# Conv inputs, q, k and v by seven-product iterations ahead of the gates, and attention inside the pool and conv projection

## The reference, cut to what matters

```python
h = _rmsnorm(x, norm1)
proj = einsum('bsd,de->bse', h, w_in)          # 2048 -> 11336 columns
(u_pool, c_b, c_c, c_x,                        # 512 columns each
 q, k, v,                                      # 1024 each: 8 heads of 128
 qi, ki, wi, gate_logits) = split(proj)        # 512, 64, 8, 6144
a = _multiscale_pool(u_pool, pool_w, pool_scale)
bconv = c_b * causal_conv3(c_c * c_x)          # along the tokens, per channel
q = _rmsnorm(q.reshape(B, S, 8, 128), q_gain)  # k likewise
c = _sparse_attention(q, k, v, qi, ki, wi * 8 ** -0.5, topk=128)
g = sigmoid(gate_logits).reshape(B, S, 3, D)
merged = g0 * (a @ w_pool_out) + g1 * (bconv @ w_conv_out) + g2 * (c @ w_attn_out)
x = x + merged @ w_o
x = x + square(relu(_rmsnorm(x, norm2) @ w_ff1)) @ w_ff2
```

## Time and profile before

| | us |
|---|---|
| median of three runs | 2642.54 |
| span of the profiled execution | 2643.3 |
| PE busy (2623.1 us) | 99% of the span |
| DVE busy (1949.0 us) | 74% |
| ACT busy (1241.7 us) | 47% |
| DMA, mean | 216 GB/s |

### The profile page before, as it was taken

One profiled execution on the slowest core, in us unless ns is written; L12 is line 12 of the kernel. 1 busy time (PEld: TensorE's weight loads), 2 busy tenths in 40 slices (PEclk: granted clock), 3 DMA queues, 4 the chain that ended last, 5 costly groups with the idle time before them and its releaser, 6 DMA issues.

```text
span 2643.3 us, 36093 instructions
## 1 busy us (share of the span) xinstructions
PE 2623.1 (99%) x14114; PEld 2255.0 (85%) x14114; DVE 1949.0 (74%) x2293; ACT 1241.7 (47%) x1615; POOL 94.5 (4%) x116
## 2 busy tenths in 40 slices
PE   8999999999999999999999999999999999999999
PEld 6688877777888888888889999999999788888887
DVE  4565654567777775477569888888887988888887
ACT  6322344335444543234566665656655433333333
POOL 0022222100000000000000000000000000000000
PEclk9999999999999999999999999999999999999999
DMA  7589999956445557556775566566568777685753
GB/s 242 174 230 247 252 254 255 275 175 236 161 160 175 175 175 271 165 169 219 251 231 174 174 211 209 166 218 198 171 219 326 256 273 251 215 318 182 273 188 121
DMA packets 317973, 570.76 MB, mean 216 GB/s; under 512 B 20137, under 2 KB 128297, under 8 KB 317297
## 3 DMA queue, kind: packets, MB, share of 16 engines
q1 hardware_dynamic: 272688, 433.64, 49.4%
q0 software_dynamic: 20736, 58.73, 9.9%
q10 hardware_dynamic: 24384, 76.18, 7.8%
HBM read 476.05 MB, written 151.01 MB: 237 GB/s over the span
## 4 chain that ended last, share of the span: by engine, by line
PE 91%; DVE 4%; DMA 3%; issue 1%; ACT 1%; SPq 0%; ACTq 0%; DVEq 0%
PE aux L1182 8%; PE aux L1184 8%; PE aux L1183 8%; PE main L1286 7%; PE main L1288 7%; PE main L1287 7%; PE main L1182 6%; PE main L1184 6%; PE main L1183 6%; PE main L511 5%; PE main L513 5%; PE main L512 5%; PE main L1217 1%; PE aux L1217 1%; PE aux L1218 1%; PE aux L1219 1%
## 5 line engine op out<-in xcount | busy, mean ns | idle before, releaser
L1286 PE MATMUL main<-sf,f_wh 128*128 128x256 f32 x1728 | 489.3, 283 | 1.1 <-ACT keeps L1773 0.9
L1287 PE MATMUL main<-sf,f_wh 128*128 128x256 f32 x1728 | 489.0, 283 | 0.0
L1288 PE MATMUL main<-sf,f_wl 128*128 128x256 f32 x1728 | 489.0, 283 | 0.0
L1286 PEld LDWEIGHTS main<-sf,f_wh 128*128 128x128 f32 x1728 | 331.7, 192 | 1.8 <-ACT keeps L1773 1.3
L1288 PEld LDWEIGHTS main<-sf,f_wl 128*128 128x128 f32 x1728 | 331.7, 192 | 0.0
L1287 PEld LDWEIGHTS main<-sf,f_wh 128*128 128x128 f32 x1728 | 331.7, 192 | 0.0
L486 DVE TENSOR_TENSOR w_lo<-w_raw,w_hi 128x512 fp32r<-128x512 f32 (+1 forms) x184 | 123.2, 674 | 207.6 <-ACT w_hi L479 206.5
L479 ACT ACTIVATE w_hi<-w_raw 128x512 fp32r<-128x512 f32 (+1 forms) x184 | 113.1, 617 | 269.3 <-PE main L513 209.0
L511 PE MATMUL main<-act_hi,w_hi 128*128 128x512 f32 x576 | 229.9, 399 | 8.0 <-DVE w_lo L486 7.9
L1473 ACT ACTIVATE f_wh<-group 128x1024 fp32r<-128x1024 f32 x128 | 135.7, 1061 | 204.9 <-PE aux L1184 104.1
L513 PE MATMUL main<-act_hi,w_lo 128*128 128x512 f32 x576 | 225.2, 391 | 0.0
(11 more groups left out here) (311 smaller groups left out, 5887.0 us busy)
## 6 DMA issues: line engine op xcount, KB each, us to landing
group<-w_ff SPq DMA_DIRECT2D x160, 512.0 KB, 5.2
f1raw<-w_ff SPq DMA_DIRECT2D x126, 512.0 KB, 5.7
sf<-f_dram ACTq DMA_DIRECT2D x56, 1024.0 KB, 11.7
group_g<-w_in SPq DMA_DIRECT2D x100, 512.0 KB, 4.6
w_raw<-w_in SPq DMA_DIRECT2D x87, 512.0 KB, 8.2
f_dram<-piece_hi SPq DMA_DIRECT2D x112, 256.0 KB, 4.0
f_dram<-piece_lo SPq DMA_DIRECT2D x112, 256.0 KB, 5.1
t_dram<-w_o POOLq DMA_DIRECT2D x48, 512.0 KB, 8.2
```

The source lines that it names most:

```text
L1286: pe.matmul(part, hi_at(8, k)[:, cols], sh, start=first, stop=False, skip_group_check=True)
L1287: pe.matmul(part, hi_at(8, k)[:, cols], sl, start=False, stop=False, skip_group_check=True)
L1288: mm = pe.matmul(part, lo_at(8, k)[:, cols], sh, start=False, stop=last, skip_group_check=True)
```

## The change

Four iterations J = -4 to -1 are put ahead of the gates: `J_CONV` makes c_c and c_x, `J_Q`, `J_K`, `J_V` make q, k, v. c_b stays plain (two passes, 16 units), which now follow the pool passes. The index scores move 9 units later, the pool product and its spill into the c_b passes. The `h` block sums are made during the index passes and `h_dram` is gone; J = 0 is an ordinary iteration; POOL's sets are 10, one for each 16 granules from granule 28 on. z = c_c c_x is multiplied with tokens on partitions; z, q and k are then turned by PE (80 transposes of 128 by 128) and spilled, v is scaled and spilled. The squares of q and k heads are summed by ACT, eight activations of 128 columns with a sum for each block where a gate block has two of 512. Top-k, masks and the convolution go between the `lo2` of the gate iterations. The gate blocks `gb` have one set of buffers, not two. The branch order becomes pool and conv for all four chunks (32 units), then attention for all four (32 units); the heads run one in four units from unit 5 on. Pool and conv segments after the first all use `main`, since attention holds `aux`.

```diff
+    J_CONV, J_Q, J_K, J_V = -4, -3, -2, -1
+    J0 = J_CONV
...
-        gb = [[at(f"gb{p}_{i}", [P, 2, S], F32, o * KB) for i, o in enumerate(at_kb)]
+        gb = [at(f"gb{i}", [P, 2, S], F32, (128 + 4 * i) * KB) for i in range(4)]
...
+        SEGS = [(ci, b) for ci in range(4) for b in range(2)] + [(ci, 2) for ci in range(4)]
+        SEG_END = [4 * s + 3 for s in range(8)] + [39 + 8 * i for i in range(4)]
...
+        def weight_cols(J):
+            if J < 0:
+                return ((c_c, PW), (c_q, S), (c_q + AW, S), (c_v, S))[J - J0]
+            return c_gate + (J % 3) * D + (J // 3) * S, D // 2
```

SP at the start of the branches (and the PE order of the iterations and branches):

```diff
+            sp.wait_ge(g_done, KO + 28 * 6)
             load_sig(0)
+            sp.wait_ge(vm_spilled, 80)
+            sp.dma_start(maskB[:], mask_dram).then_inc(rows_landed[6], 16)
             load_sig(1)
+            sp.wait_ge(vm_spilled, 64)
+            sp.dma_start(vv[:], v_dram.rearrange("t p c -> p t c")).then_inc(rows_landed[5], 16)
             next_sig = 2
             for g in range(u_b + 8, u_w, 2):
                 load_b(g)
...
-            for J in range(6):
-                for n, g in order_of(J):
+            for J in range(J0, 6):
+                for idx, (n, g) in enumerate(order_of(J)):
                     granule(J, n, g)
+                    if J == J_Q and idx in (5, 7):
+                        for i in range(2):
+                            turn_block(idx - 5 + i)
+                    if J in (J_K, J_V) and idx in (3, 5, 7):
+                        for i in ((0, 1, 2, 3), (4, 5), (6, 7))[(idx - 3) // 2]:
+                            turn_block(tile_0(J) + i)
...
+            for ub in range(4 * KT):
+                a = ub - ATTN_AT
+                h, s = a // 4, a % 4
+                if 0 <= a <= 4 * ATTN_HEADS and s == 0:
+                    if h:
+                        pv(h - 1)
+                    if h < ATTN_HEADS:
+                        logits(h)
+                if 0 <= a < 4 * ATTN_HEADS and s == 3:
+                    turns(h)
...
+                branch_unit(ub)
```

ACT: the end of an iteration, and the way of the k factors through DRAM:

```diff
-            def sigmoid_gate(J, i):
+            def finish_gate(J, i):
+                if J == J_CONV:
+                    return
...
+                    if J in (J_Q, J_K):
+                        for c in range(4):
+                            n = 32 * (J - J_Q) + 8 * i + 4 * j + c
+                            col = 4 * (8 * (J - J_Q) + 4 * v + c) + t
+                            if n >= 2:
+                                act.wait_ge(hq_squared, n - 1)
+                            act.activation(head_junk[n % 2][:], gb[blk][:, j, c * P:(c + 1) * P], ACT.Square,
+                                           accum_out=ss64[:, col:col + 1]).then_inc(hq_squared, 1)
...
+                    if J == 1 and idx == 0:
+                        act.wait_ge(k_ready, 1)
+                        act.dma_start(k_dram.rearrange("h (t p) -> p h t", p=P),
+                                      rqk[:, 32:64].rearrange("p (h t) -> p h t", t=TT),
+                                      allow_slow_non_contiguous=True).then_inc(k_moved[0], 16)
...
+                if ub == 1:
+                    load_k_factor(0)
+                    load_k_factor(1)
```

DVE: the end of the plain passes, what is put between the granules' splits, and the branches:

```diff
+            def cb_evict(i):
+                dve.wait_ge(unit_done, (6 + i) * UP)
...
+                for m in range(2):
+                    ins = dve.tensor_tensor(cbT[i][:, m], main[:, bank + m, :], rB[:, :], ALU.mult)
...
+            cb_evict(1)
...
+            TOP_AT = [(J, idx) for J in range(J0, 2) for idx in (6, 9, 11, 13, 15, 17, 19) if J > J0 or idx > 6]
+            def mixers_after(J, idx):
+                if (J, idx) in TOP_AT:
+                    pick_top(UP - 1 + TOP_AT.index((J, idx)))
...
+                if J == 2 and idx in (9, 13, 17):
+                    chain.step(mask((idx - 9) // 4))
+                if J in (3, 4) and idx in (9, 14):
+                    convolve(2 * (J - 3) + (idx == 14))
...
+            mix_t1(J0, 0)
+            for J in range(J0, 6):
                 for g in range(4):
                     lo2(J, 0, g)
...
+                if ub == 3:
+                    scale_k(0)
+                if ub - 1 in SEG_END[:8] and SEGS[SEG_END.index(ub - 1)][1]:
+                    merge_sums(SEG_END.index(ub - 1))
...
+                if ub in SEG_END:
+                    merge(SEG_END.index(ub))
```

POOL:

```diff
-            for n in range(14 + 3):
-                    pool.wait_ge(lo_ready, u_qk + 8 * n)
+            for n in range(10 + 3):
+                    pool.wait_ge(f_lo, 28 + 16 * n)
```

More of the change, by code:

```diff
@@ L754, in _ @@
                 load_b(g)
-                while next_sig < 12 and 4 * next_sig + 4 * (next_sig // 3) <= (g - u_b - 8):
+                while next_sig < 12 and SEG_END[next_sig - 2] + 4 <= g - u_b - 8:
                     load_sig(next_sig)
@@ L1214, in _ @@
                 pe.wait_ge(lo_ready, g + 1)
                 for t in range(TT):
+                    if first and s >= 2 and s != 10:
+                        pe.wait_ge(gate_mul, 4 * (9 if s == 11 else s - 1) + t + 1)
                     th, tl = brT[:, kt, 0, t * P:(t + 1) * P], brT[:, kt, 1, t * P:(t + 1) * P]
@@ L1606, in _ @@
                     gates_after(J, idx)
+                    if J == J_Q and idx in (9, 12):
+                        for i in range(2):
+                            tile_out((idx - 9) // 3 * 2 + i)
+                    if J in (J_K, J_V) and idx in (6, 7, 9, 12):
+                        for i in range(2):
+                            tile_out(tile_0(J) + 2 * (6, 7, 9, 12).index(idx) + i)
+                    if J == 0 and idx == 8:
+                        act.wait_ge(ms_ready, 2)
+                        act.activation(rqk, ms64, ACT.Sqrt).then_inc(root_done, 1)
@@ L1968, in pool_group, with clear_scores @@
                                   ALU.subtract).then_inc(pool_diff, 1)
-            for g in range(u_idx, u_qk):
+            def clear_scores():
+                dve.wait_ge(score_added, 24)
+                for i in (1, 2, 3):
+                    chain.step(dve.memset(score[i - 1][0:CHUNK, i * P + CHUNK:(i + 1) * P], EMPTY))
+                chain.wait()
+                for i in (1, 2, 3):
+                    chain.step(dve.tensor_copy(work[i - 1][:], score[i - 1][:]))
+                chain.wait()
@@ new lines, in pick_top @@
+            def pick_top(pair):
+                t = pair % 3
+                chain.step(dve.max(top8[t], work[t][:]))
+                chain.wait()
+                chain.step(dve.match_replace(work[t][:], top8[t], work[t][:], EMPTY))
+                chain.wait()
+            def cb_evict(i):
+                dve.wait_ge(unit_done, (6 + i) * UP)
+                if i == 0:
+                    dve.wait_ge(score_added, 24)
+                    dve.wait_ge(pool_diff, NW)
+                else:
+                    dve.wait_ge(a_spilled[0], 64)
+                bank = 2 * (1 - i)
+                for m in range(2):
+                    ins = dve.tensor_tensor(cbT[i][:, m], main[:, bank + m, :], rB[:, :], ALU.mult)
+                ins.then_inc(cb_ready, 1)
+                dve.wait_ge(cb_ready, i + 1)
+                dve.sem_inc(set_free[1 - i], 1)
@@ L2056, in mask @@
                 kth = top8[t][:, 7:8]
[L2057 removed]
+                above, equal, rank = dst, work[t][:], score[t][:]
                 chain.step(dve.tensor_scalar(above, score[t][:], kth, None, ALU.is_gt, ALU.add,
@@ new lines, in convolve @@
+            def convolve(m):
+                if m % 2 == 0:
+                    dve.wait_ge(conv_landed, 16 * m + 32)
+                if m == 0:
+                    dve.wait_ge(vm_spilled, 80)
+                else:
+                    dve.wait_ge(b_lo, m)
+                tap = [cst[:, C_CW + 4 * k + m:C_CW + 4 * k + m + 1] for k in range(CONV_K)]
+                chain.step(dve.tensor_scalar(yc[:], zz[:, m % 2, 0:S], tap[0], None, ALU.mult))
+                for k in range(1, CONV_K):
+                    chain.wait()
+                    chain.step(dve.scalar_tensor_tensor(yc[:], zz[:, m % 2, k:k + S], tap[k], yc[:], ALU.mult, ALU.add))
+                chain.wait()
+                dve.tensor_tensor(yc[:], yc[:], cbl[:, m % 2], ALU.mult).then_inc(b_ready, 1)
```

1367 lines of the change are left out of this document (616 added, 751 removed).

## The result

The changed kernel takes 2653.4 us (median of 4) where the kernel before takes 2643.0: the ratio is 1.004, with an interval from 1.0028 to 1.0053. So it is slower by 10 us where I forecast 33 us less.

What follows compares the result with a forecast made beforehand. The prediction took PE as the bound, busy 2623.1 of 2643.3 us. Its terms, -43.6 - 7.3 + 9.1 - 3.6 + 5.7 + 3.2 + 3.0, gave -33.5 us: 2609 us, range 2603 to 2616 (0.60), eight in ten 2599 to 2625.

Steps and rivals of the forecast that it cites:

- scattered write: J = 1, k factors written as 4096 single floats: 36 us to land, delaying a copy 7 us (2616); chance 0.04, taken as 0.
- GpSimd's rounds: POOL's block-sum sets beside group loads in J = -3 to 2: no cost in the sum, a cost only if DMA fills up.
- sign that I had named for being wrong: Either `g_wl` waits all over the gates (DVE or DMA late), or a wait at every head.
- What PE has to do: Matmuls removed and added net -43.6 us, squares' sums -7.3 us, turns of tiles +9.1 us.
- Turns: 80 transposes on PE for 20 tiles: 0.105 us each, 8.4 us, plus 0.7 for matmuls behind groups, together +9.1 us.
- Old stalls that go: Gates, nearly all in J = 0, 2.8 us of stall and 0.8 for the spill of h disappear: -3.6 us.
- Start of J = -4: First granule waits for DVE's c_b products, sum and low part: 4.0 us idle plus 1.7 from low clock, 5.7 us.
- Squares on ACT: End of J = -3 and -2: eight squares take 3.1 us, 1.9 more than two sigmoids; PE loses 3.2 us in all.
- DVE's added work in the iterations: Top-k, masks and convolution between splits: DVE 86 to 88% busy, covered by the splits' lead, costed at nothing.
- Branches and later heads: Head 0 waits behind k factor, merge and unit 8's weights: 3.0 us (first 1.4); later heads add nothing.
- DMA fills up: Group loads beside POOL's sets in J = -3 to 2: 57 loads late by 1.1 us each, 63 us, 2672; chance 0.04.

Runs made afterwards that it cites:

- k_before: Kernel before the change plus the same write of 4096 single floats on ACT's queue at J = 1, read by nobody: 2650.6 us, ratio 1.0025.
- a_kturn: Changed kernel with k factors turned by DVE in 32 x 32 blocks and written as 128 runs of 128 bytes: 2639.5 us, ratio 0.9983.
- c_wo: Changed kernel with W_o's first four weight blocks ahead of the reloads of x in SP's queue: 2643.7 us, ratio 0.9997.
- g_all: Changed kernel with five mends (k write, W_o order, unit 8's weights, J = -4 start, spread GpSimd DMAs) and two k factors fetched earlier: 2602.3 us, ratio 0.9842.
- f_spread: Changed kernel with the eight DMAs of each GpSimd round issued one per two granules, not all at once: 2634.7 us, ratio 0.9971.

## Why the prediction was wrong

The step that failed is the pricing of DMAs beside the iterations and ahead of W_o. The sum has 0 for the scattered write ("As small as that data is, I take 0") and 0 for GpSimd's rounds, and no term for the reloads of x ahead of W_o's weights. The runs showed 17.1 us of loss at the write and a round beside it, 19.9 at two bursts of the rounds and 8.9 at W_o. Neither sign that I had named for being wrong showed: `g_wl` waits stand in four places and not all over the gates, and no later head waits. Term by term:

**What PE has to do: right.** The first and the last matmul are 9.4 us further apart than before, the loss grew by 56.7, so by this count the work shrank by 47.3 where the sum had 41.8. The difference is no gain. The line of the index scores mixes three shapes, and its median is 0.289 us before and 0.157 after, though its 48 instructions take 10.9 us together before and 10.2 after. With one price for each kind and shape in both kernels the work shrank by 42.6 us and the loss grew by 52.0. Turns came at 0.109 us each.

**Old stalls that go: right at least.** By that count the loss outside the places of the table fell by 9.3 us where I had 3.6. Most of the rest is a stall that nothing in the change aims at and that I don't explain: from 2000 us on, in the MLP, the loss is 5.0 us before, around the wait of the earlier trace rows, and 0.6 after.

**Start of J = -4: right in mechanism and size.** 4.1 us of wait, then half the clock, 7.2 in all against 5.7.

**Squares on ACT: mechanism right, price too high.** I took 0.39 us for a square with its sum and 3.1 for eight. The row is 0.29 us, and eight take 327.19 - 324.83 = 2.36:

```profile
324.83 0.31 ACT L1456 ACTIVATE head_junk<-gb 128x128 f32<-128x128 f32 x1 [3.56 <-DVE gb L2142]
...
327.19 1.04 ACT L1417 ACTIVATE g_wh<-tx_g 128x1024 fp32r<-128x1024 f32 x1
...
328.26 1.23 DVE L2085 TENSOR_TENSOR g_wl<-tx_g,g_wh 128x1024 fp32r<-128x1024 f32 x1 [3.47 <-ACT g_wh L1417]
```

The low part is done at 329.49, and PE, which loses nothing there, takes it at 329.54. The lead of 2.1 us of the earlier trace rows was eaten down to 0.05, which just sufficed; that nothing was lost is in part luck.

**DVE's added work in the iterations: right**, at nothing. From 251.8 to 328 us, nearly all of J = -3 with turns, top-k pairs and squares in it, PE does not pause, with DVE busy for 82% of the time (I had 86 to 88):

```profile
251.80:328.00 76.20, 76.20 (x345) 63.22 (x344) 62.82 (x70) 36.38 (x65) 4.84 (x6) 1.00 0.70 208
```

**Branches and later heads: right in mechanism, under-sized for head 0.** The waits stand where the text put them, at the first logits behind k factor and merge and at the first turns behind unit 8's weights, and no later head waits. The first was 3.2 and not 1.4, because merge's first product starts 8.5 us after the k factor is asked for and the four take 2.5, and a slow clock follows, which I left out: 7.9 us against 3.0.

**The scattered write: named, and thrown away.** It had a chance of 0.04 and a price of 7 us. Its own length was overstated (36 us against 18.1), but the step that failed is who waits for it. I looked along ACT's queue, at when the spills behind it land and at the copy that waits for them. In the changed kernel the waiting was done by group loads of another queue, for while the write runs the DMA engines stand at a share of about 1 and it carries 16 KB. In `k_before` it was done by ACT itself, held 6.1 us at the issue of a spill, a cost that I had not thought of. Alone the write costs 7.7 us (`k_before`), here 13.9 (`a_kturn`). The Trainium skill, DMA: Bandwidth & Descriptors, "Rules for kernel authors", asks for a contiguous last dimension because each element becomes a descriptor. The traces agree: from 645 to 668 us of `k_before`, 4112 packets belong to the queue that carries the write, whose elements are 4096. I should have given that sentence more than 0.04. The same skill, VectorE: DVE Perf Modes, "The three transpose paths", says that DVE turns blocks of 32 x 32 only; here that is what was needed, as runs of 128 bytes landed in at most 9.5 us (`a_kturn`).

**DMA fills up: the right rival with the wrong arithmetic.** I gave it 0.04, on the ground that between 120 and 400 us loads had such neighbours at a share of 1.0 and PE did not wait. That was read from the wrong place (the rounds of the kernel before run from 111 to 450 us): those loads were of plain units, and by the waits in the kernel's code such a load is issued seven units ahead of its split, an estimated 19 us and not 10.9. And I took means, a round's 18.7 us over 43.6, and one class of landing time for all loads. What happens is that the eight DMAs of a round start at once and the group loads and spills issued beside them need 15 to 18 us instead of 5, some of them longer than PE's other work covers; the rest are hidden. So it cost two waits and 20 us of loss, and not 57 waits and 63 us. I also did not weigh the spills of tiles, whose four buffers give them less time than group loads have.

**The start of W_o: missed.** I put nothing for it and gave no reason. The change makes the branches' segments in another order and moves the splits of merged's first half from units 42 to 54 to units 52 to 61, and I followed neither of them to SP's queue, where the reloads of x wait for them and W_o's weights stand behind: 8.9 us of loss, and 9.7 us of time in `c_wo`.

In short, forecast and result are 33.5 + 10.4 = 43.9 us apart. Of these 17.1 are the loss around 602 us (the scattered write and a round beside it), 19.9 the two other bursts, 8.9 the order at W_o, 4.9 a head 0 and 1.5 a start of J = -4 that were under-sized; the squares give back 2.9, PE's own work 0.8 and the loss elsewhere 5.7. That makes 42.9; the other 1.0 is the difference between the profiled executions (9.4 us slower) and the medians (10.4). That `g_all` lands below the forecast's 2603 by only 1 us doesn't prove the sum: it also takes away the start of J = -4 (5.7) and most of the start of the branches (3.0), which the sum had left in. But the gain in products was there all the time.

## What to carry to other kernels

When work is moved, list the waits at the head of each queue that it passes, and for each DMA ask what else is on the DMA engines at that moment, whichever queue it comes from. A DMA of very small pieces is priced by the pieces and not by its bytes (18.1 us for 16 KB here), and those that pay are the neighbours' loads with the shortest lead and the engine that issues the next DMA. Here a burst from a background queue was better issued one DMA at a time, paced by the main loop (18.7 us less), than moved (18.0 us more).

## What the runs showed of the hardware that I had not expected

4096 writes of 4 bytes took 17.4 to 18.1 us, the four writes of 32 rows of 128 bytes at most 9.5 us beside the same loads, and during the first, in `k_before`, the DMA share read 1.27 at 81 GB/s. An engine can be held by issuing a DMA: ACT for 6.1 us in `k_before`. The matmuls behind waits of 3.2 us and more ran at half the clock (1.2 GHz) for some microseconds; so did those behind a wait of 1.9 us in `g_all` (432 to 436 us, mean clock 0.57). Those behind the waits of at most 1.7 us in `k_before` did not (clock 1.00). With the slow clock behind them, the gaps of 4.3 and 3.9 us at 171 and 519 us of the changed kernel cost 7.2 and 6.8, one of 4.4 in `f_spread` 5.9.
